# A sample's window keys are requested ahead of its cache pages, and the first pages are spread over the output projection's weight chunks

## What is computed

```python
h = rms(x, norm_w) * (1 + scale) + shift            # shift, scale, gate from silu(c) @ w_ada + b_ada
z = h @ w_in                                        # MLA q | MLA kv | 3 groups of dilated q, k, v | gates
a = mla(...)       # prompt: causal; sample: over 32 cache pages of 128 rows of [latent 256 | rotary 32]
b = dilated(...)   # windows (128,1), (512,4), (2048,16), combined by their softmax denominators
y = x + gate * ((sigmoid(ma) * ((a * silu(ga)) @ w_pa) + sigmoid(mb) * ((b * silu(gb)) @ w_pb)) @ w_out)
```

## Time and profile before

| | |
|---|---|
| median of 3 runs | 1314.69 us (1312.73 to 1319.53) |
| the profiled execution | 1309.67 us, its span 1307.8 us |
| mean granted TensorE clock | 0.95 of full speed |
| TensorE busy | 1133.9 us (87%) |
| VectorE busy | 699.2 us (53%) |
| ScalarE busy | 504.2 us (39%) |
| GpSimd busy | 256.7 us (20%) |

### The profile page before, as it was taken

How to read it: one execution, slowest core, us unless ns; L and a number is a source line. 1 busy time by engine, 2 the same in 40 slices (tenths; PEclk the granted TensorE clock), 3 DMA queues, 4 the chain that set the end, 5 groups by cost and what they waited for, 6 DMA issues and landing times.

```text
span 1307.8 us, 23020 instructions
## 1 busy us (share of the span) xinstructions
PE 1133.9 (87%) x7578; PEld 955.9 (73%) x7578; DVE 699.2 (53%) x1618; ACT 504.2 (39%) x1180; POOL 256.7 (20%) x263
## 2 busy tenths in 40 slices
PE   5998759998898999999978779998999899981997
PEld 1267647886776777787757778988898889881873
DVE  4317887356855550401245466766676667652761
ACT  1323545243253543323324434445454545440430
POOL 0033350147857123334320000000000000000000
PEclk9998869999999999999988989999999999995999
DMA  8542010031242122332453420323232323232042
GB/s 274 188 127 72 25 44 1 17 81 45 77 129 88 39 79 80 101 84 76 147 160 100 120 106 19 87 85 93 70 87 84 94 74 88 81 94 74 1 146 98
DMA packets 82016, 115.49 MB, mean 88 GB/s; under 512 B 8907, under 2 KB 57180, under 8 KB 81901
## 3 DMA queue, kind: packets, MB, share of 16 engines
q1 hardware_dynamic: 78790, 104.73, 27.4%
q0 software_dynamic: 1472, 5.13, 1.0%
q10 hardware_dynamic: 1648, 4.23, 0.9%
HBM read 108.35 MB, written 5.70 MB: 87 GB/s over the span
## 4 chain that ended last, share of the span: by engine, by line
PE 52%; DVE 13%; issue 12%; SPq 8%; ACT 5%; POOL 5%; DMA 5%; DVEq 0%; ACTq 0%; POOLq 0%
PE ps L1468 13%; PE ps L1128 6%; PE ps L1130 6%; PE ps L1129 6%; PE ps L1449 4%; SPq L543 3%; SPq L540 3%; DVE ssq L2331 3%; PE ps L1494 2%; DMA raw<-in_w_ada 2%; PE ps L1143 2%; ACT cT_hi L930 2%; PE ps L1273 1%; PE ps L1267 1%; POOL wlo L1004 1%
## 5 line engine op out<-in xcount | busy, mean ns | idle before, releaser
L1004 POOL TENSOR_TENSOR wlo<-raw,whi 128x512 fp32r<-128x512 f32 (+3 forms) x148 | 171.6, 1164 | 403.4 <-ACT whi L668 403.3
L1468 PE MATMUL ps<-wq_hi,cT_hi 128*128 128x260 f32 x1024 | 218.5, 295 | 1.0 <-ACT sq L959 1.0
L1128 PE MATMUL ps<-whi,hT_hi 128*128 128x512 f32 (+3 forms) x512 | 189.3, 370 | 28.7 <-POOL wlo L1004 19.7
L1468 PE MATMUL ps<-wq_hi,cT_lo 128*128 128x260 f32 x1024 | 206.7, 283 | 0.0
L1468 PE MATMUL ps<-wq_lo,cT_hi 128*128 128x260 f32 x1024 | 206.7, 283 | 0.0
L668 ACT ACTIVATE whi<-raw 128x512 fp32r<-128x512 f32 (+3 forms) x148 | 82.9, 564 | 313.3 <-PE ps L1125 246.9
L2331 DVE TENSOR_REDUCE ssq<-sq 128x8 f32<-128x512 f32 x256 | 172.1, 682 | 55.9 <-ACT sq L959 49.0
L1130 PE MATMUL ps<-whi,hT_lo 128*128 128x512 f32 (+3 forms) x512 | 185.3, 362 | 0.0
L1129 PE MATMUL ps<-wlo,hT_hi 128*128 128x512 f32 (+3 forms) x512 | 185.1, 362 | 0.0
L1468 PEld LDWEIGHTS ps<-wq_hi,cT_hi 128*128 128x128 f32 x1024 | 158.3, 191 | 1.6 <-ACT sq L959 1.6
L1468 PEld LDWEIGHTS ps<-wq_hi,cT_lo 128*128 128x128 f32 x1024 | 158.8, 189 | 0.0
(11 more groups left out here) (408 smaller groups left out, 1540.5 us busy)
## 6 DMA issues: line engine op xcount, KB each, us to landing
cn<-in_cache_mla SPq DMA_DIRECT2D x256, 144.0 KB, 2.1
raw<-in_w_in SPq DMA_DIRECT2D x64, 256.0 KB, 2.7
raw<-in_w_ada SPq DMA_DIRECT2D x48, 256.0 KB, 3.1
raw<-in_w_in SPq DMA_DIRECT2D x32, 128.0 KB, 2.0
raw<-in_w_out SPq DMA_DIRECT2D x16, 256.0 KB, 2.9
w_out_s<-in_w_out SPq DMA_DIRECT2D x8, 512.0 KB, 7.3
tab<-in_cw SPq DMA_DIRECT2D x24, 128.0 KB, 2.4
queries_spread<-queries_by_sample SPq DMA_DIRECT2D x8, 384.0 KB, 4.3
```

Source lines behind the costliest of these rows:

```text
L1004: nc.gpsimd.tensor_tensor(out=wlo[:, s % NHL, 0:width], in0=raw[:, j % NRAW, 0:width], in1=whi[:, s % NHL, 0:width].bitcast(F32), op=ALU.s ...
L1128: mm(out, hi[:, k, c], bh, start=st, stop=False)
L1468: last = mm(ps[:, 3 + 2 * (u % 2) + f, 0:260], a[c], wq[:, c, f, w], start=c == 0 and a is hi and wq is wq_hi, stop=c == 1 and a is lo)
```

## The change

Four things differ. (1) In SyncE's loop over the chunks of the output block, the number of pages after a chunk j (its number in the whole list; the block's chunk 7 is number 187, its last is 195) is 1 + j % 2 instead of 4, and pages of sample 0 that are left over are requested after the last chunk. (2) The keys of samples 0 and 1 are requested ahead of the pages of sample 1; in the loop the wait for `kwin_read` and the keys stand ahead of the pages. (3) ScalarE's two waits stand after the rotary copies of the first two groups of sample 0 instead of ahead of them. (4) VectorE's preparation of constants stands at the end of `sample_gates`, between the two output halves, instead of after them.

```diff
             for j in range(FIRST["WO0"] + NHL + NRAW, len(CHUNKS)):
                 stream_to(j + 1)
-                for _ in range(4):
+                for _ in range(1 + j % 2):
                     if n < NPAGE:
                         load_page(0, n // 8, n, n)
                         n += 1
+            while n < NPAGE:
+                load_page(0, n // 8, n, n)
+                n += 1
             sp.wait_ge(z_done, LAST_ITEM["WO1"] + 1)
             sp.wait_ge(y_out[1], 16)
...
+            for p in range(2):
+                load_keys(p, p)
             for quarter in range(4):
                 with sp.Fori(0, 8) as u:
                     load_page(1, quarter, NPAGE + 8 * quarter + u, 8 * quarter + u)
             sp.dma_start(wuvr[:, :, :], w_uv.rearrange("(k p) n -> p k n", p=P)).then_inc(wuv_in, 16)
-            for p in range(2):
-                load_keys(p, p)
...
                 for p in range(2):
+                    sp.wait_ge(kwin_read, 2 * i + p + 1)
+                    load_keys(p, 2 * i + 2 + p)
                     for quarter in range(4):
                         with sp.Fori(0, 8) as u:
                             load_page(p, quarter, 2 * NPAGE * i + (2 + p) * NPAGE + 8 * quarter + u, 8 * quarter + u,
                                       2 * i + p)
-                    sp.wait_ge(kwin_read, 2 * i + p + 1)
-                    load_keys(p, 2 * i + 2 + p)
...
-            act.wait_ge(stage_free, staged[0])
-            act.wait_ge(y_out[0], 16)
-
...
                     if g == 0 and first:
                         rotary_keys(8 * b, 0, p, turn)
                         rotary_keys(8 * b + 1, 1, p, turn)
+                        act.wait_ge(stage_free, staged[0])
+                        act.wait_ge(y_out[0], 16)
                         hi_rows(b * 8, 0)
...
                 link(v.memset(x4[:, :], 0.0))
+                link(v.tensor_tensor(out=sel[:, :], in0=ident[:, 0:8], in1=ident[:, 40:48], op=ALU.add))
+                link(v.tensor_tensor(out=sel[:, :], in0=sel[:, :], in1=ident[:, 80:88], op=ALU.add))
+                link(v.tensor_tensor(out=sel[:, :], in0=sel[:, :], in1=ident[:, 120:128], op=ALU.add))
+                for n in range(2):
+                    link(v.tensor_tensor(out=halves[:, NB * n:NB * n + NB], in0=ident[:, 32 * n:32 * n + NB],
+                                         in1=ident[:, 64 + 32 * n:64 + 32 * n + NB], op=ALU.add))
+                link(v.memset(SD_t[:, :], NEG))
                 v.memset(flag[:, :], 0.0).then_inc(gates_ready, 1)
```

More of the change, by code:

```diff
@@ L2160, in _ @@
             v.memset(Sc[:, NPAGE, :], NEG)
[L2161 to L2167, removed]
             base = [0]
```

## The result

The changed kernel takes 1263.8 us (median of 4 runs, 1263.46 to 1264.67) against 1315.31 us (4 runs, 1312.73 to 1319.53): a ratio of 0.9606, 95% interval 0.958 to 0.9633, so 3.9% faster. The profiled execution took 1264.04 us, 45.6 us less than the profiled one of before (1309.67), which was a short one of its kind. Some executions of a kernel have a prompt phase some 25 us longer at a lower granted clock (among them the profiled ones of the first and the fourth experiment, of which only later stretches are read); medians and ratios are given without them.

A forecast was written before the change was run, and what follows sets the result against it. SyncE's requests were taken to bound the output block, and SyncE's order to cause the two long waits. 11.2 + 0.7 + 12.2 + 30.1 = 54.2 us off the 1314.69 us median gave 1260.5, stated as 1260, range 1250 to 1275.

The forecast's parts named there:

- Output block: Fewer pages among the weight chunks: SyncE's requests hidden by matmuls, last chunk at 671.2 instead of 682.40, 11.2 us gained.
- The new wait at chunk 11: Output block: GpSimd's store of the first half delays splitting chunk 11, so TensorE waits 1.8 us.
- The rule that speaks against it: Skill's rule that initiating a DMA is usually small beside the transfer: spreading requests in the output block would gain nothing.
- the rival that transfers bound the block: Output block: the same bytes move no faster, so no 11.2 us there; 1271.7 us, chance 0.09.
- Start of the samples: ScalarE's two waits moved behind the first rotary copies: the high half begins earlier, 0.7 us gained.
- Sample 0: Keys ahead of sample 1's pages: VectorE's 10.82 us wait for queries and slow TensorE work go, 12.2 us gained.
- Sample 7: Keys ahead of pages in the loop: the last sample's 28.96 us wait and slow TensorE work go, 30.1 us gained.
- Pages of sample 7: Loop: pages asked no later than before and ready in the first group, costing nothing.
- scores' wait: Loop: waiting for earlier scores ahead of pages costs nothing; rival that it holds every sample's pages, 1351 us, chance 0.03.
- tail of pages: Behind the output block's last chunk: 20 pages end at 682.4, hidden by the second output store's wait until 684.
- the covers at nothing: Sample 7's pages, the scores' wait and the pages behind the last chunk: hidden under other waits, each costed at zero.
- VectorE's constants: Six small operations and a memset moved into the output block: costed at nothing, about 1.4 us if uncovered.

The follow-up runs named there:

- the first and the fourth experiment: Kernel before with page spreading alone, 1301.67 us, ratio 0.9894; and with ScalarE's waits and VectorE's constants moved alone, 1314.8 us, ratio 0.9974.

## Why the prediction was right, and where it was off

It was right in the whole, 1260 for 1263.8 and inside 1250 to 1275, and in the mechanism of each part. Point by point:

- **Output block**: 11.2 us said, 10.8 measured, here and in the kernel with that part alone. The new wait at chunk 11 was forecast at 1.8 us and came at 1.96, for the reason given; the experiment that took the store out of the way removed it. From ScalarE's chunk 10 to the end of chunk 11's split it is again 10.2 us (653.17 to 663.34, 662.08 plus a third of 3.76).
- **The rule that speaks against it**: the Trainium skill, "DMA: Bandwidth & Descriptors", section "Issuing engines are not separate DMA queues", has the time to initiate a DMA as usually small beside the transfer. Here pages of 144 KB followed one another at 1.11 us, two, three and four in a row (1.46, 2.58 and 3.68 us less 0.35 for the last), against 0.44 us estimated for their data, so the row was the better guide, and the rival that transfers bound the block is out. But the prediction set the page's sentence against all of the 1.12 us, and only 0.35 of them initiate the DMA. That is about as long as the data take, though small against the 2.1 us from issue to landing; the larger part is the reading of the page's number, of which the sentence says nothing.
- **Start of the samples**: 0.7 said, 0.6 and 0.5 measured.
- **Sample 0**: 12.2 said, 12.8 and 13.0 measured, 11.8 and 12.0 against the second trace of before. The halved clock behind the wait had cost 2.2 us, not the 1.35 that I put down: the products behind the transposes were slow for longer.
- **Sample 7**: 30.1 said, 28.2 measured. Here a term was wrong. I let 0.85 us of slow transposes and 0.3 us of products go with the wait, though I kept 4.1 us of waiting in the same place. The wait is 3.98 us, and behind it the transposes still take 1.94 us: here the halved clock followed a wait of 4 us as it had followed one of 33 us. It even lasted longer. The windows of 6 us from the transposes on, first before, then changed:

```profile
1206.39:1212.39 6.00, 6.00 (x39) 6.00 (x40) 3.10 (x7) 2.12 (x5) 0.00 (x0) 0.74 0.01 3
1156.13:1162.13 6.00, 6.00 (x31) 6.00 (x32) 3.10 (x7) 1.69 (x3) 0.00 (x0) 0.57 0.35 101
```

A clock of 0.74 and 0.57 is 3.1 and 5.2 us at half speed (an estimate from the two levels). So of the 33.04 - 3.98 = 29.1 us of wait that went, 0.9 came back, where I had added 1.15: that is the whole miss. With three pages a chunk the same wait of 3.98 us was followed by transposes of 1.22 us, since the clock fell only behind most of them, and that group took 9.8 us. With waits of 1.42 us and less they take 1.06 or 1.07. The fall of the clock came with the rest of the wait, and did not go with the part that went.
- **Pages of sample 7, scores' wait, tail of pages** (the covers at nothing): the first two held. The middle stretch is 409.3 us against 409.4. The 20 pages behind the last chunk ended at 688.0, where I had 682.4; 3.1 us of that are the longer prompt phase. The keys left right behind them (688.21), so the wait for the second store covered them no more, which I had allowed for, and it cost nothing. VectorE's constants cost nothing either; they are five sums and a memset, not six and a memset as the prediction has it.
- **The tail**: not in the sum at all, and it took 3.7 us. Its instructions are the same, and what differs is the clock. Windows of the tail (us, busy us of PE, PEld, DVE, ACT, POOL, granted clock, DMA share, GB/s), first before, then changed, five stretches of 4 us from the same matmul on:

```profile
1277.73:1281.73 4.00, 1.74 (x17) 1.09 (x20) 1.93 (x5) 0.42 (x1) 0.00 (x0) 0.94 0.72 238
1281.73:1285.73 4.00, 4.00 (x52) 2.15 (x48) 0.00 (x0) 0.00 (x0) 0.00 (x0) 0.63 1.01 410
1285.73:1289.73 4.00, 3.29 (x54) 2.20 (x45) 0.92 (x5) 0.00 (x0) 0.00 (x0) 1.00 0.35 139
1289.73:1293.73 4.00, 3.63 (x24) 1.07 (x24) 0.16 (x1) 0.00 (x0) 0.00 (x0) 1.00 0.02 4
1293.73:1297.73 4.00, 2.73 (x20) 2.17 (x22) 0.92 (x2) 0.00 (x0) 0.00 (x0) 1.00 0.00 0
```

```profile
1228.38:1232.38 4.00, 1.74 (x13) 1.19 (x16) 1.93 (x5) 0.42 (x1) 0.00 (x0) 0.65 0.73 249
1232.38:1236.38 4.00, 4.00 (x42) 1.78 (x36) 0.00 (x0) 0.00 (x0) 0.00 (x0) 0.50 0.98 381
1236.38:1240.38 4.00, 3.35 (x42) 2.02 (x35) 0.89 (x4) 0.00 (x0) 0.00 (x0) 0.93 0.38 157
1240.38:1244.38 4.00, 3.62 (x41) 2.10 (x43) 0.19 (x1) 0.00 (x0) 0.00 (x0) 0.50 0.01 4
1244.38:1248.38 4.00, 3.67 (x16) 0.77 (x8) 0.22 (x1) 0.00 (x0) 0.00 (x0) 0.72 0.00 0
```

In the first window TensorE is busy for 1.74 us in both, but it gets through 17 matmuls in the one and 13 in the other. Up to the matmuls at L1491 (L1493 now) both did the same work with the same waits, of 0.63 and 1.64 us, and these start 2.84 and 2.83 us into the window. They already take 0.59 us instead of 0.39:

```profile
1280.57 0.39 PE L1491 MATMUL ps<-esm,ones 128*128 128x8 f32 x2 [1.64 <-DVE esm L2267]
1231.21 0.59 PE L1493 MATMUL ps<-esm,ones 128*128 128x8 f32 x2 [1.64 <-DVE esm L2269]
```

The clock was granted at 0.94 in that window before and at 0.65 now, and was at 0.50 in two later ones. Over the 14 traces this tail was 35.7 us in four, 36.4 in three, and 39.4 to 43.1 in the other seven. What decides it was not tried by itself and stays open. It came out the same in two traces of before and in two of the changed kernel, and differed when a stretch ahead of it changed by a few microseconds, as with three pages a chunk (36.4 where the changed kernel has 39.4). When the tail begins, counted from the kernel's start, does not decide it alone: in the two traces of before it began at 1267.73 and at 1270.83 us and took 35.69 both times.

The prompt phase's 3.1 us are the difference between two executions: a second trace of the kernel before has them too. That is part of why the sum came out nearer against the median (54.2 said, 51.5 measured) than against the two profiled executions (45.6). That 1260 lies so near 1263.8 owes a little to chance too: sample 0 came out 0.6 us over its term and sample 7 1.9 under it.

## What to carry to other kernels

In a queue whose issuing engine works in order, look at what each request stands behind, and put the small one that is wanted first ahead of the long row that is wanted later; here that was worth 41 of the 52 us and cost nothing, because the engine had idle time at its next wait. Where requests stand between others that feed a busy engine, compare the time that the issuing engine needs for all of them (here 0.43 + n x 1.12 us, of which the reading of page numbers is the larger part) with that engine's time for one piece (2.80 us), not the bytes. When a wait is shortened but not removed, leave what follows a wait, such as a halved clock, in the sum until the rest of the wait is short too.

## What the runs showed of the hardware that was not expected

VectorE was held up whole by GpSimd. In the changed kernel GpSimd splits three chunks without a break, from 662.08 to 665.84, and VectorE's four copies of the merge gates, 2.57 us before, take 5.05 us, 3.75 of them the first, which ends at 666.12, just behind the third split (665.84), and takes 0.42 where no split runs; the second of the constants' sums takes 1.23 us beside a split that starts at 670.07, where its neighbour takes 0.17. VectorE's timeline:

```profile
662.37 5.05 DVE L2143 COPY merge_gates_by_group<-merge_gates_held 8x512 f32<-8x512 f32 x4
...
669.95 0.17 DVE L2148 TENSOR_TENSOR sel<-tab 128x8 f32<-128x8 f32 x1
670.15 1.23 DVE L2149 TENSOR_TENSOR sel<-sel,tab 128x8 f32<-128x8 f32 x1
```

The 1.23 us end where that split of 1.29 us ends. The Trainium skill, "SBUF — State Buffer", section "Terms", describes a pair of ports that VectorE and GpSimd hold in turn for a whole instruction, the other being blocked fully; by that rule the small sum waits for the split's end, and the trace agrees. It cost nothing here, since VectorE had 3.9 us left before the second half's tiles, but the constants could not have been moved beside GpSimd's splits for free where VectorE is the bound.

The other surprise is how much of this kernel's run-to-run spread is TensorE's clock in stretches that nothing was done to: 8 us in the prompt phase, and up to 7.4 us in the tail between programs, where the other stretches repeat to 1.5 us at worst and mostly to some tenths. Stretches between equal matmuls told the 10.8, 0.6, 12.8 and 28.2 us of the parts from one another; medians of whole runs could not tell 3 us.
